# A 31-tap depthwise convolution is shared between VectorE and TensorE, with diagonals of taps made by GpSimd

## The reference, cut to what matters

```python
def causal_dwconv(x, w, b):          # w: K taps by C channels
    K, C = w.shape
    y = lax.conv_general_dilated(
        x, w[:, None, :], window_strides=(1,), padding=[(K - 1, 0)],
        dimension_numbers=("NWC", "WIO", "NWC"), feature_group_count=C)
    return y + b

def conformer_conv(x, norm, w1, b1, dw_w, dw_b, ln_g, ln_b, w2, b2):
    h = rms_norm_2(x, norm) @ w1 + b1
    h = jax.nn.glu(h, axis=-1)
    h = causal_dwconv(h, dw_w, dw_b)          # K = 31, C = 1024
    h = jax.nn.silu(layer_norm_2(h, ln_g, ln_b))
    return h @ w2 + b2
```

## Time and profile before

| | us |
|---|---|
| median of 3 executions | 1998.99 |
| lowest and highest | 1995.81, 1999.39 |
| the profiled execution, its own time | 1998.05 |
| its span, first to last instruction | 1995.9 |
| its mean granted TensorE clock | 0.950 of full |

### The profile page before, as it was taken

How to read it: one execution, slowest core, us unless ns; L and a number is a source line. 1 busy time by engine, 2 the same in 40 slices (tenths; PEclk the granted TensorE clock), 3 DMA queues, 4 the chain that set the end, 5 groups by cost and what they waited for, 6 DMA issues and landing times.

```text
span 1995.9 us, 26512 instructions
## 1 busy us (share of the span) xinstructions
PE 1794.4 (90%) x10479; PEld 1588.8 (80%) x10479; DVE 1231.1 (62%) x1661; ACT 1030.6 (52%) x1389; POOL 32.6 (2%) x58
## 2 busy tenths in 40 slices
PE   6799999999999999999899699999999307989998
PEld 6688888877888888888689688899999206879997
DVE  3564766656546476565757555566665995546665
ACT  4655555454656555645464655555455104545544
POOL 4000000000000000000000000000000000000000
PEclk9989999999999999999999899999999657989999
DMA  7345545555453454555554353455655102335563
GB/s 255 95 148 169 165 135 185 166 169 198 152 168 127 148 168 136 185 162 177 179 162 140 127 197 112 151 185 168 203 179 180 43 21 93 118 116 183 167 206 110
DMA packets 161915, 306.73 MB, mean 154 GB/s; under 512 B 12323, under 2 KB 16325, under 8 KB 161665
## 3 DMA queue, kind: packets, MB, share of 16 engines
q1 hardware_dynamic: 158928, 298.91, 46.2%
q0 software_dynamic: 2864, 6.14, 0.9%
HBM read 303.97 MB, written 1.05 MB: 153 GB/s over the span
## 4 chain that ended last, share of the span: by engine, by line
PE 75%; DVE 14%; ACT 8%; issue 2%; POOL 0%; DMA 0%; DVEq 0%; ACTq 0%; POOLq 0%
PE bank L1449 42%; PE bank L1467 26%; DVE arena L1360 4%; DVE weights_lo L915 3%; ACT weights_hi L485 1%; PE bank L1760 1%; ACT arena L502 1%; PE bank L1742 1%; DVE h_lo L952 1%; PE bank L1531 1%; ACT spatial_weights L512 0%; PE bank L1489 0%; DVE arena L1179 0%; ACT arena_parts L549 0%; DVE arena_parts L958 0%
## 5 line engine op out<-in xcount | busy, mean ns | idle before, releaser
L915 DVE TENSOR_TENSOR weights_lo<-weights_raw,weights_hi 128x1024 fp32r<-128x1024 f32 x562 | 675.0, 1222 | 550.6 <-ACT weights_hi L485 548.0
L485 ACT ACTIVATE weights_hi<-weights_raw 128x1024 fp32r<-128x1024 f32 x562 | 583.1, 1055 | 499.3 <-PE bank L1449 336.4
L1467 PE MATMUL bank<-h_hi,weights_hi 128*128 128x256 f32 x1504 | 434.0, 289 | 41.2 <-DVE weights_lo L915 21.5
L1467 PE MATMUL bank<-h_hi,weights_lo 128*128 128x256 f32 x1504 | 431.3, 287 | 0.0
L1467 PE MATMUL bank<-h_lo,weights_hi 128*128 128x256 f32 x1504 | 431.2, 287 | 0.0
L1449 PE MATMUL bank<-weights_hi,h_hi 128*128 128x512 f32 x928 | 372.5, 401 | 36.8 <-DVE weights_lo L915 20.1
L1449 PE MATMUL bank<-weights_lo,h_hi 128*128 128x512 f32 x928 | 367.5, 396 | 0.0
L1449 PE MATMUL bank<-weights_hi,h_lo 128*128 128x512 f32 x928 | 366.9, 395 | 0.0
L1467 PEld LDWEIGHTS bank<-h_hi,weights_hi 128*128 128x128 f32 x1504 | 294.7, 196 | 45.3 <-DVE h_lo L952 18.7
L1449 PE MATMUL bank<-weights_hi,arena_parts 128*128 128x512 f32 x928 | 294.8, 394 | 34.0 <-DVE weights_lo L915 34.0
L1467 PEld LDWEIGHTS bank<-h_hi,weights_lo 128*128 128x128 f32 x1504 | 295.1, 196 | 0.4
(11 more groups left out here) (286 smaller groups left out, 1375.8 us busy)
## 6 DMA issues: line engine op xcount, KB each, us to landing
weights_raw<-in_w_in_dram SPq DMA_DIRECT2D x224, 512.0 KB, 3.9
weights_raw<-in_f_w_up_dram SPq DMA_DIRECT2D x96, 512.0 KB, 4.4
weights_raw<-in_f_w_down_dram SPq DMA_DIRECT2D x48, 512.0 KB, 4.1
weights_raw<-in_w_up_dram SPq DMA_DIRECT2D x40, 512.0 KB, 4.2
weights_raw<-in_c_w_pw_dram SPq DMA_DIRECT2D x24, 512.0 KB, 3.8
weights_raw<-in_ab_w_in_dram SPq DMA_DIRECT2D x20, 512.0 KB, 3.7
weights_raw<-in_w_mem_kv_dram SPq DMA_DIRECT2D x16, 512.0 KB, 3.7
weights_raw<-in_w_out_dram SPq DMA_DIRECT2D x16, 512.0 KB, 3.8
```

The lines of the kernel that those rows point to most:

```text
L485: nc.scalar.activation(w_hi[:, q % SPLIT, 0:w], raw[:, n % RAW, 0:w], ACT.Copy).then_inc(hi_done, 1)
L915: tt(w_lo[:, q % SPLIT, 0:w], raw[:, n % RAW, 0:w], w_hi[:, q % SPLIT, 0:w].bitcast(F32), ALU.subtract)\
L1467: ins = mm(bs[i][:, j, :], wp[:, kk, f * P:(f + 1) * P], sp_[:, 2 * u + kk, :], start=first and u == us[0] and kk == 0 and n == 0 and j == ...
```

## The change

TensorE takes tiles 5, 6 and 7: a tap is a product with a 128 x 128 diagonal matrix of that tap's 128 weights, and 31 such products add up in a bank. GpSimd makes the 31 diagonals of a tile (the identity times a column of weights), 4 sections of the arena: tile 5's after the product oT 3 of stage X0, tile 6's after o 3 of stage F0, and tile 7's in the place of tile 5's, once PE is through with tile 5. ACT copies the three banks into y with the bias. DVE has tiles 0 and 1 as a pair, begun after glu 1, and then 2, 3 and 4 in turns. glu 2 and 3 stand inside the taps of the first pair. The splits are placed anew. v is cut in two halves around mu, and ACT's copies of v now stand behind rstd. The two additions to x_tokens stand behind the taps.

```diff
@@ order of PSUM tiles, stage C
-                      + pick("ca", 2, 3) + pick("v", 0, 1) + pick("mu", 0) + pick("var", 0) + four("o"))
+                      + pick("ca", 2, 3) + pick("cv", *CONV_PE) + pick("v", 0, 1) + pick("mu", 0) + pick("var", 0) + four("o"))
@@ GpSimd
+            def diagonals(ft):
+
+                for d in range(31):
+                    c = COL_C + 48 + 8 * (30 - d) + ft
+                    ins = nc.gpsimd.tensor_scalar(diag(ft)[:, d, :], ident, cols2[:, c:c + 1], 1.0, ALU.mult, ALU.mult)
+                ins.then_inc(pool_done, GC(f"diag{ft}"))
...
+            pool.wait_ge(pe_done, PC.at(("oT", 3), "X0"))
+            diagonals(5)
+            pool.wait_ge(pe_done, PC.at(("o", 3), "F0"))
+            diagonals(6)
+            pool.wait_ge(pe_done, PC.at(("cv", 5)))
+            diagonals(7)
@@ ScalarE
-                for ft in range(4 * n, 4 * n + 4):
+                for ft in range(4 * n, 4 + n):
...
-            for i in range(2):
-                copy(v[:, i, 0:512], "v", i, ACT.Copy)
+            for ft in CONV_PE:
+                b = filled("cv", ft)
+                link(nc.scalar.activation(feat(16, 2)[:, ft, :], b[:, 0:S], ACT.Identity,
+                                          bias=cols2[:, COL_C + 24 + ft:COL_C + 25 + ft]), ("free", "cv", ft), f"cv{ft}")
             log_exp_table()
             for u in range(4):
                 act.wait_ge(vec_done, after_vec(f"cen{u}"))
...
+            for i in range(2):
+                copy(v[:, i, 0:512], "v", i, ACT.Copy)
@@ VectorE
+            def taps(fts, between):
+
+                dve.wait_ge(act_done, after_act(f"tap{fts[-1]}"))
+                for d in range(1, 31):
+                    between(d)
+                    for ft in fts:
+                        c = w0 + 8 * (30 - d) + ft
+                        stt(y[:, ft, d:S], feat(2, 2)[:, ft, 0:S - d], cols2[:, c:c + 1], y[:, ft, d:S], ALU.mult, ALU.add)\
+                            .then_inc(vec_done, VC(*([f"dw{ft}"] if d == 30 else [])))
+                        dve.wait_ge(vec_done, VC.n + 1 - len(fts))
+
+            def first_taps(d):
+                if d % 2 == 0:
+                    past("ca", 1, min(4 + d // 2, 10))
+                if d in (22, 24):
+                    glu(d // 2 - 9)
+
+            def more_taps(d):
+                past("ca", 3, min(d // 3, 1 + SPLIT))
+
+            glu(0)
+            glu(1)
+            taps((0, 1), first_taps)
+            dve.wait_ge(vec_done, VC.n)
+            taps((2, 3, 4), more_taps)
+            dve.wait_ge(vec_done, VC.n)
             dve.wait_ge(brow_in, 8 * 16)
             for t in range(NT):
                 link(tt(xs[:, t, :], xs[:, t, :], brow[:, 0:D], ALU.add))
...
+            dve.wait_ge(act_done, after_act("cv7"))
@@ TensorE
-            proj_T("v", 0, src=M_HL["X"])
+            for ft in CONV_PE:
+                pe.wait_ge(pool_done, GC.at(f"diag{ft}"))
+                pe.wait_ge(vec_done, VC.at(f"glu{ft}"))
+                b = begin("cv", ft)
+                for d in range(31):
+                    ins = mm(b[:, d:S], diag(ft)[:, d, :], feat(2, 2)[:, ft, 0:S - d], start=d == 0, stop=d == 30,
+                             skip_group_check=True)
+                end(ins, "cv", ft)
+            proj_T("v", 0, src=M_HL["X"], us=(0, 1), last=False)
             b = begin("mu", 0)
             for k in range(KD):
-                pe.wait_ge(vec_done, VC.at(f"dw{k}"))
+                if k in CONV_PE:
+                    pe.wait_ge(act_done, SC.at(f"cv{k}"))
+                else:
+                    pe.wait_ge(vec_done, VC.at(f"dw{k}"))
                 ins = mm(b[:, 0:S], ones, feat(16, 2)[:, k, :], start=k == 0, stop=k == KD - 1)
             end(ins, "mu", 0)
+            proj_T("v", 0, src=M_HL["X"], us=(2, 3), first=False)
```

More of the change, by code:

```diff
@@ L196, in pick, with diag @@
             return [(name, i) for i in at]
+        CONV_PE = (5, 6, 7)
+        DIAG = {5: 18, 6: 8, 7: 18}
+        def diag(ft):
+            return sec(DIAG[ft], 4).rearrange("p (d n) -> p d n", n=P)
         GATES = lambda b: two(f"yT{b}") + four(f"gate{b}", f"up{b}")
@@ L468, in _ @@
             pool.dma_start(brow[:, 0:D], A["c_b_pw2_2"].to_broadcast([P, D])).then_inc(brow_in, 16)
+            def diagonals(ft):
[3 more added lines that the diff above has]
+                ins.then_inc(pool_done, GC(f"diag{ft}"))
             pool.dma_start(brow[:, D:2 * D], A["final_norm_2"].rearrange("(a d) -> a d", a=1).to_broadcast([P, D]))\
                 .then_inc(brow_in, 16)
+            GC.enter("C")
+            pool.wait_ge(pe_done, PC.at(("oT", 3), "X0"))
[4 more added lines that the diff above has]
+            diagonals(7)
         @block.scalar
@@ L1338, in _, with glu @@
             low_part(COL_C, cols2)
-            for i in range(4):
+            def glu(i):
                 b = halves(filled("ca", i))
@@ L1345, in _ @@
                              ALU.add, ALU.mult), f"glu{ft}", *([("free", "ca", i)] if j else []))
-                if i == 1:
-                    for_tile("cb", 3)
+            w0 = COL_C + 48
+            y = feat(16, 2)
+            def taps(fts, between):
[20 more added lines that the diff above has]
+            dve.wait_ge(vec_done, VC.n)
             dve.wait_ge(brow_in, 8 * 16)
@@ L1350, in _ @@
                 link(tt(xs[:, t, :], xs[:, t, :], brow[:, 0:D], ALU.add))
[L1351 to L1362, removed]
             dve.wait_ge(vec_done, VC.n)
```

## The result

| | before | after |
|---|---|---|
| median, us | 1997.40 (4 executions) | 1977.18 (4 executions) |
| lowest and highest | 1994.71, 1999.39 | 1976.3, 1980.01 |
| span of the profiled execution | 1995.9 | 1974.5 |

The ratio is 0.990, with a 95% interval of 0.9887 to 0.9918: 20.2 us less, between 16.4 and 22.6. The forecast was 1978.5, 20 us less.

A forecast was written before the change was run, and what follows sets the result against it. VectorE's taps were taken to set the conformer stage's end. Var's reader gains 21.5 us, 0.4 goes back, net 21.1, less 1 for earlier stretches: 20 us, giving 1978.5 us, range 1966 to 1992 (chance 0.80).

The forecast's parts named there:

- Part 1: VectorE's early taps of tiles 0 and 1: glu5 there at 1556.5, pair ended at 1564.3, mostly hidden under TensorE's projection.
- Part 2: TensorE's tiles 5 to 7: idle 7.4 us before tile 5, clock lost; tiles end at 1571.8, 1584.4 and 1597.0.
- Part 3: GpSimd's diagonals: 0.35 us each, 10.9 for 31; tile 7's hidden under tile 6, turns with taps delaying tile 7 about 1 us.
- the prediction's own signs of being wrong: Taps without the hole, GpSimd releasing tile 7's first product, or granted clock of 0.50 within tiles 6 and 7.
- slow-GpSimd rival: Tile 7's diagonals at c us each add 31c - 12.6 us; 1 to 1.5 us gives 1997 to 2012; chance 0.08 above 0.84.
- Part 4: VectorE at tap 12 of tiles 2 to 4 waits some 24 us for ScalarE's high half of v's weights; taps end 1623.8.
- Part 5: To the stage's end: reader of mu 22.5 us earlier, reader of var 21.5 earlier, net 21.1, less 1: 20 us.
- the wait isn't there: Rival: ScalarE's high half comes without VectorE's wait at tap 12; 44 us gained at var's reader, time 1956; chance 0.05.
- the rival of the half clock: TensorE stays at half clock through the diagonal products, 25.1 us a tile; time 2013, slower than before; chance 0.05.

The follow-up runs named there:

- e1_ahead: Changed kernel with ScalarE's high half put ahead of its copies of tiles 5 to 7, VectorE asking for that unit only: 1964.32 us, ratio 0.9844.
- e6_unbroken: As e1_ahead, with VectorE's split at tap 2 of tiles 2 to 4 instead of tap 12: 1980.6 us, ratio 0.992.
- e2_quiet: Changed kernel with VectorE's taps 1 to 11 of tiles 2 to 4 left out, nothing else: 1975.71 us, ratio 0.9896.
- e5_v_first: As e1_ahead, plus tile 7's diagonals made by ScalarE, v's first half before tile 5, its second between tile 7 and mu: 1948.66 us, ratio 0.9767.

## Why the prediction was right

Point by point, by its own steps. *Part 1* held: glu5 was foretold for 1556.5 and ended at 1556.75. *Part 2*: tile 5 began at 1556.85 and the two tiles took 28.5 us (27.9 foretold); ACT read tile 6 at 1585.42 (1584.4). The clock was lost in the gap, as assumed: 0.50 in 1553 to 1563, full from 1563 on, 6.1 us after the products began where 5 was foretold; so tile 5 took 15.9 us (15.3 foretold; by the sum's own 5 us at half clock it would be 15.1) and tile 7 12.9.

*Part 3* had the price of the operation right (0.35 us, from two rows of other operations) and the contention wrong. It said that GpSimd and the taps would take turns until DVE stops, with a loss of 1 us, beside the rule of the Trainium skill, SBUF — State Buffer (Who interferes with whom), that a DVE instruction with two SBUF inputs and a GpSimd instruction that reads SBUF exclude each other. Its sum took nothing for it. The trace agrees that the two get in each other's way, but not in this form. In the changed kernel the first diagonal was held for all the 4.8 us until DVE stopped, through 13 taps and not through one, and tile 7 began 3.0 us late. And behind the split of e1_ahead 30 diagonals and 31 taps fitted into 14.8 us, which is less than the 22 us that whole instructions one after the other would need. With that, one of the prediction's own signs of being wrong was there: GpSimd is the releaser of tile 7's first product. Set 7 took 15.46 us, 0.50 apiece, and the rule of the slow-GpSimd rival (31c - 12.6) gives 2.9 us for it; but the price of the operation was not slow, one instruction was held.

*Part 4* was the step that decided, and it held to the tap: idle at tap 12, released by ACT's high half of B+11, 26.65 us of idle time. The 24 of the prediction included the split itself, so 23 is what compares, and 3.0 of the difference are those of Part 3. That the position could be counted from the code, and checked against the places of the four splits in the trace of before, is what made it safe. *Part 5*: the reader of mu was to be 22.5 us earlier and was 18.8 (19.3 from glu); that of var 21.5, and was 18.1. The mu products took 4.81 us (5.2), since the clock came back in them.

Up to the output projection, the stage gave 17.8 us (1665.35 to 1647.57), 3 less than the sum, and the median gave 20.2. Behind that projection nothing was edited, and yet the profiles take 320.4 to 324.9 us from there to the last DVE group, without order: 324.9 before, 321.2 after, 324.5 in e1_ahead and 320.4 in e6_unbroken. So part of the agreement to 1.3 us is luck; 18 us is inside the interval (16.4 to 22.6).

The rival *the wait isn't there* was priced at 1956. With the wait gone the time was 1964.32: its mechanism was the missing wait alone, and it left out what e1_ahead showed, that set 7 then runs beside the taps. With that taken away too, 1953. The clock was 1.00 from 1563 to 1600 in tiles 5 to 7, so the rival of the half clock did not occur; nor did slow GpSimd as an operation (30 diagonals in 10.4 us).

## What to carry to other kernels

When work is moved to another engine, ask what each queue waits for in its new order: here ScalarE's copies stood in front of a high half that VectorE needed, and 27 us of idle time were the price. Two faults can hide each other: the hole that cost 27 us was also the time in which GpSimd could work, so the first repair returned only half, and the same repair with a split ten taps earlier left mu's reader 5 us later than no repair (110.96 against 106.01 us from glu). Small preparations that must be made beside a dense run of two-input VectorE instructions are better on ScalarE than on GpSimd, if ScalarE is idle there as it was here (set 7: 9.18 us against 22.81).

## What the runs showed of the hardware

A GpSimd tensor_scalar of 128x128 fp32 costs 0.35 us while VectorE is silent (30 in 10.4 us), a ScalarE activation of the same 0.30 (31 in 9.18 us). Beside scalar_tensor_tensor with both tensors in SBUF, a GpSimd instruction that reads SBUF was held for 5.02, 8.05 and 28.99 us, each time until the run of taps was broken: by idle time in the first case, by a tensor_tensor in the others (a split, and the additions to x_tokens). Behind the split both advanced, at 0.49 us a diagonal and 0.48 us a tap.

A tensor_tensor with both inputs in SBUF holds GpSimd too. In set 6 of the changed kernel one diagonal lasted 2.48 us, from 1495.51 to 1497.99, beside two splits back to back that ran from 1495.47 to 1497.83. Sets 5 and 6, made among such splits, took 15.7 and 15.8 us, where set 7 of e2_quiet took 10.77 with VectorE silent. So it is not shown that the kind of instruction is what let GpSimd in behind the single split of e1_ahead. Why a break is needed for GpSimd's first instruction there, but not for the next ones, stays open: no run was made with a pause of another kind.

In the kernel before, TensorE stopped at 1557.5 and its granted clock was 0.81 in 1561 to 1563; it stopped at 1590.7, after 6 us of work, and the clock was 0.98 in 1592 to 1593 and 0.50 in 1593 to 1594. Plain fp32 products with mostly zero weights kept it at 1.00 for 30 us (1563 to 1593 in e5_v_first).
